# Queries as extra columns of the key products, absorbing products on column groups, and a new step order in a decoder-layer kernel

## The chip, the cores and the metric

The kernel runs on one core of a Trainium2 chip. The metric is device time in microseconds of one execution of the whole program; lower is better. The core has TensorE (PE in the profile, its weight loads PEld), VectorE (DVE), ScalarE (ACT), GpSimd (POOL) and a queue that issues DMAs (SP).

## What is computed

One layer of a decoder for 256 prompt tokens and 8 sequences with 4 new tokens each, in float32: an input projection, an mLSTM branch, a branch of latent attention (MLA), a merge, and a convolutional FFN. The change lies in the MLA branch. For the samples it computes, per sequence, over 1024 cached positions and the new ones:

```python
def mla_keys(c_kv, k_rope, w_uk, g_kn, g_kr):
    k_nope = jnp.einsum('...sc,chd->...shd', c_kv, w_uk)          # 512 latent -> 16 heads x 128
    k_r = jnp.broadcast_to(k_rope[..., None, :], k_nope.shape[:-1] + (B_ROPE,))
    return qk_norm(k_nope, k_r, g_kn, g_kr)                       # RMS norm of each head's 192 entries

def mla_attend(q, k, c_kv, mask, w_uv):
    s = jnp.einsum('bqhe,bkhe->bhqk', q, k).astype(jnp.float32) * ATTN_SCALE
    s = jnp.where(mask, s, -jnp.inf)
    p = jax.nn.softmax(s, axis=-1).astype(c_kv.dtype)
    o_lat = jnp.einsum('bhqk,bkc->bqhc', p, c_kv)
    return jnp.einsum('bqhc,chv->bqhv', o_lat, w_uv)
```

## The kernel before

**Precision.** A large product is made of three in the type fp32r: both operands are split into a high part (suffix H or hi) and a low part (L or lo), and hi·hi, hi·lo and lo·hi are added up in one PSUM bank. Small products are plain f32.

**Page loop (lines 1322 to 1880).** The cache of a sequence is 8 pages of 128 positions (`NPG`), and there are 8 sequences (`NB`): 64 pages. The keys' RMS norm needs the squares of all 16 heads' keys, so PE computes the keys of each page: `keys(b, j)` multiplies the page's turned latents (`latH`, `latL`, as weights) with `w_uk` (`ukH`, `ukL`, as moving columns) in 4 groups of 512 columns (4 heads), each group 4 chunks times 3 products in a PSUM bank of its own (0 to 3). ACT squares a group (`squares`, L1627), and DVE sums it per head (`sums`, L1701). The scores don't use these keys: the queries were multiplied with `w_uk` beforehand (`qlat`: 16 heads x 4 queries = 64 columns, high and low part), and `scores(b, j)` multiplies the same latents with 128 columns (L1480, high times both parts) and 64 columns (L1481, low times high), four of each, and adds the rotary part (L1482, f32, 64 rows of weights). Its bank 5 is folded by DVE (`fold`, L1709) into the buffer `sc`. For each page PE runs: `turn(b, j + 1)` (five f32 transposes of the next page, L1452 and L1453), `keys`, `scores`, and one small step for the sequence before (maxima, denominators, values L1555, turn_out L1560). After a sequence's 8 pages `scale` on DVE divides by the norms and takes maxima; for the last sequence this, the softmax and the value product come at the end with nothing beside them.

**Key loop of the prompt (L793 to 808 and the functions above it).** For `h` in 0 to 18, PE does: `keys(h)` (head h of the prompt's keys, L718, four f32 products of 288 columns), `flip(h - 2)` (transposes of one head of `w_uk`, L728), `absorb(h - 3)` (L736: 32 columns of sample queries as weights, 512 moving columns of the turned `w_uk`, f32, output on the 32 rows `(h % 4) * 32` of bank 6), every second head `key_sums` (L750), and every fourth `absorbed` (L743). DVE copies each turned head out of PSUM (`flipped`, L1232, two buffers), adds and inverts norms (`key_norm` L1236, `key_inverse` L1242) and copies four absorbed heads (`absorbed`, L1247). ACT copies and squares keys, and takes roots (`key_root`, L1014).

**Prompt attention.** Before it come two products with `w_uv`, new keys and the scores of four heads. Then for eight pairs of heads `step(p)`: `turn_p(2p)` (L859), `values(2p - 1)` (L869, L870), `turn_p(2p + 1)`, `values(2p)`, and after the step `scores(p + 2)` (L845, L849) and, in the first four, `values_of` (L829: 512 columns, f32). `turned_p`, `exps`, `scaled` and `out` are ACT's part, `soft` and `norm_` DVE's.

The order of work on an engine is the order of the code; engines meet at semaphores (`wait_ge`, `need`). The rest of the kernel (the projections, blocks of 288-column products at L298, L299, L303) is not touched.

## Time and profile before

| | |
|---|---|
| three runs | 2988.29, 2986.86, 2981.94 us; median 2986.86 us |
| the profiled execution | 2982.09 us, its span 2980.3 us |
| PE busy | 2918.2 us, 98% of the span |
| DVE, ACT busy | 1435.8 us (48%), 1121.8 us (38%) |
| granted TensorE clock, mean | 0.993 of 2.4 GHz |
| key loop and prompt attention | about 145 to 303 us |
| page loop | about 318 to 1184 us |

A PE row stands for a product with its drain; neighbours overlap, so the time that a product takes of PE is the distance between two starts, not its length. A plain f32 product appears as two rows. "PEld" rows are the loads of weights, which run beside products.

### The profile page before, as it was taken

How to read it: one execution, taken by the hardware profiler on the slowest of the kernel's cores; microseconds unless marked ns; L12 is line 12 of the kernel's file. 1: busy time of each engine (PE TensorE's matmuls, PEld its weight loads, DVE VectorE, ACT ScalarE, POOL GpSimd, SP SyncE). 2: the span in 40 equal slices, each digit the busy share in tenths (PEclk: the TensorE clock that was granted, in tenths of full speed). 3: DMA queues.
4: the chain of work that ended last, by engine and by line, in shares of the span. 5: the costliest groups of instructions: out<-in, count | busy, mean ns of one | idle time of the engine just before them, and what ended most of it. 6: DMA issues, size and time to landing. Idle time of an engine off the chain costs nothing. (4 is left out here: it accounts for less than half of the span.)

```text
span 2980.3 us, 49155 instructions
## 1 busy us (share of the span) xinstructions
PE 2918.2 (98%) x19158; PEld 2649.9 (89%) x19158; DVE 1435.8 (48%) x2153; ACT 1121.8 (38%) x1750; POOL 104.4 (4%) x346
## 2 busy tenths in 40 slices
PE   8998999999999999899999999999999999999999
PEld 7855788888888887899999999999999999999999
DVE  5464433333333333355545444445677654677644
ACT  5525322322322232354444333334444433444433
POOL 0000000000000000000000000002200000000100
PEclk9999899999999999999999999999999999999999
DMA  6512401011011001656565655556555555655564
GB/s 208 201 65 78 128 1 32 1 33 33 5 29 32 16 17 71 196 158 194 158 195 156 195 162 170 165 159 185 171 161 163 165 146 168 185 159 165 148 179 127
DMA packets 619380, 370.93 MB, mean 124 GB/s; under 512 B 23792, under 2 KB 600882, under 8 KB 618168
## 3 DMA queue, kind: packets, MB, share of 16 engines
q1 hardware_dynamic: 607032, 356.44, 40.4%
q10 hardware_dynamic: 11824, 11.50, 1.1%
q8 instruction: 109, 1.79, 0.2%
q0 software_dynamic: 368, 0.81, 0.1%
q14 instruction: 47, 0.39, 0.0%
HBM read 345.98 MB, written 22.75 MB: 124 GB/s over the span
## 5 line engine op out<-in xcount | busy, mean ns | idle before, releaser
L286 DVE TENSOR_TENSOR w_lo_b<-stage,w_hi_b 128x2048 fp32r<-128x2048 f32 (+1 forms) x289 | 619.1, 2142 | 429.1 <-ACT w_hi_b L279 429.0
L298 PE MATMUL bank<-xnH,w_hi_b 128*128 128x288 f32 x2784 | 755.9, 299 | 5.9 <-PEq L191 5.8
L299 PE MATMUL bank<-xnL,w_hi_b 128*128 128x288 f32 x2784 | 750.6, 296 | 0.0
L279 ACT ACTIVATE w_hi_b<-stage 128x2048 fp32r<-128x2048 f32 (+1 forms) x289 | 517.8, 1792 | 571.2 <-PE bank L303 536.7
L298 PEld LDWEIGHTS bank<-xnH,w_hi_b 128*128 128x128 f32 x2784 | 524.3, 188 | 18.3 <-issue 18.0
L299 PEld LDWEIGHTS bank<-xnL,w_hi_b 128*128 128x128 f32 x2784 | 523.9, 188 | 0.3
L1465 PE MATMUL bank<-ukH,latH 128*128 128x512 f32 x1024 | 405.2, 396 | 0.0
L1701 DVE TENSOR_REDUCE rk<-sq_n 128x4 f32<-128x512 f32 x256 | 175.5, 685 | 466.5 <-ACT sq_n L1627 466.5
L1467 PE MATMUL bank<-ukH,latL 128*128 128x512 f32 x1024 | 399.5, 390 | 0.0
L1466 PE MATMUL bank<-ukL,latH 128*128 128x512 f32 x1024 | 399.4, 390 | 0.0
L303 PE MATMUL bank<-xnH,w_lo_b 128*128 128x288 f32 x2784 | 396.5, 295 | 0.0
L303 PEld LDWEIGHTS bank<-xnH,w_lo_b 128*128 128x128 f32 x2784 | 378.1, 188 | 0.0
L1627 ACT ACTIVATE sq_n<-bank 128x512 f32<-128x512 f32 x256 | 153.2, 599 | 510.7 <-PE bank L1467 510.7
L298 PE MATMUL bank<-haH,w_hi_b 128*128 128x288 f32 x1024 | 278.1, 299 | 6.8 <-PEq L191 3.9
L299 PE MATMUL bank<-haL,w_hi_b 128*128 128x288 f32 x1024 | 276.6, 297 | 0.0
L1467 PEld LDWEIGHTS bank<-ukH,latL 128*128 128x128 f32 x1024 | 192.6, 188 | 40.7
L1466 PEld LDWEIGHTS bank<-ukL,latH 128*128 128x128 f32 x1024 | 193.0, 188 | 38.1
L1465 PEld LDWEIGHTS bank<-ukH,latH 128*128 128x128 f32 x1024 | 192.9, 188 | 38.1
L298 PEld LDWEIGHTS bank<-haH,w_hi_b 128*128 128x128 f32 x1024 | 194.3, 190 | 7.5 <-issue 7.3
L299 PEld LDWEIGHTS bank<-haL,w_hi_b 128*128 128x128 f32 x1024 | 195.1, 191 | 0.0
L303 PE MATMUL bank<-haH,w_lo_b 128*128 128x288 f32 x1024 | 151.9, 295 | 0.0
L303 PEld LDWEIGHTS bank<-haH,w_lo_b 128*128 128x128 f32 x1024 | 141.6, 188 | 0.0
(472 smaller groups left out, 3011.7 us busy)
## 6 DMA issues: line engine op xcount, KB each, us to landing
stage<-in_w_in_dram SPq DMA_DIRECT2D x88, 1024.0 KB, 5.2
stage<-in_w_up_dram SPq DMA_DIRECT2D x88, 1024.0 KB, 5.4
stage<-in_w_down_dram SPq DMA_DIRECT2D x64, 704.0 KB, 4.6
latf<-in_cache_kv_latent_dram SPq DMA_DIRECT2D x64, 256.0 KB, 2.5
stage<-in_w_branch_a_dram SPq DMA_DIRECT2D x16, 1024.0 KB, 5.5
stage<-in_w_branch_b_dram SPq DMA_DIRECT2D x16, 1024.0 KB, 5.5
stage<-in_w_out_dram SPq DMA_DIRECT2D x16, 1024.0 KB, 5.6
stage<-in_w_uk_dram SPq DMA_DIRECT2D x8, 1024.0 KB, 5.2
```

The source lines that it names most:

```text
L279: act.activation(h, a, ACT.Copy).then_inc(w_hi, 1)
L286: dve.tensor_tensor(lo, a, h.bitcast(F32), ALU.subtract).then_inc(w_lo, 1)
L298: pe.matmul(out, hi, xH(k), start=first and k == 0, stop=False)
L299: pe.matmul(out, hi, xL(k), start=False, stop=False)
L303: mm = pe.matmul(out, lo, xH(k), start=False, stop=last and k == kc - 1)
L1465: pe.matmul(bank[g][:], h, ukH[:, k, cols], start=k == 0, stop=False)
L1466: pe.matmul(bank[g][:], h, ukL[:, k, cols], start=False, stop=False)
L1467: mm = pe.matmul(bank[g][:], lo, ukH[:, k, cols], start=False, stop=k == LC - 1)
L1627: act.activation(sq[:, g % 2, :], bank[g][:], ACT.Square).then_inc(n_sq, 1)
L1701: dve.tensor_reduce(rk[:, b.mod(2), j, g * 4:g * 4 + 4], sq[:, g % 2, :].rearrange("p (h d) -> p h d", d=NOPE), AX.X, ALU.add).then_inc(n_ ...
```

## The change

1. **Queries as columns.** `ukH` and `ukL` get 128 columns more: two slots of 64, left and right of the first three heads. DVE copies the next sequence's `qlat` into a slot (`next_queries`, three copies, at the third page of a sequence). The page's key products now run in 5 groups: 3 heads and the queries (448 columns), three times 3 heads (384), and 4 heads (512), in banks 0, 1, 2, 3, 5. The scores fall out of group 0; `scores` and `fold` are gone, ACT copies the 64 score columns out of bank 0 before it squares the keys.
2. **Rope product first.** The rotary product (f32, 64 columns) stands at the head of group 0, right after the transposes.
3. **Absorbing products on column groups.** `absorb(j)` issues the products of four heads in a row, on the four groups of 32 output rows; the turned `w_uk` gets four buffers, two of them where `xnL` and `xnH` lie, so that `flipped(2)` and `flipped(3)` wait for the stores of those, and the store of `xnH` moves forward in SP's order. The copy of four absorbed heads moves from DVE to ACT, ahead of `key_root`.
4. **A new step order** in the prompt's attention, on PE and on ACT.
5. Some small buffers (`ol`, `hs`, `sq`) lie elsewhere.

```diff
@@ sync: the stores
-                    for i in range(6, VCH):
+                    chunk(6)
+                    sp.wait_ge(x_H, KC)
+                    sp.dma_start(xnH_dram, xnH[:].bitcast(F32)).then_inc(xH_out, 16)
+                    for i in range(7, VCH):
                         chunk(i)
-                    sp.dma_start(xnH_dram, xnH[:].bitcast(F32)).then_inc(xH_out, 16)
@@ tensor: key loop
-                    def absorb(h):
-                        g = h % 4
-                        pe.wait_ge(u_ev, h + 1)
-                        if g == 0:
-                            need(pe, u_ab, h // 4)
-                        mm = pe.matmul(bank[6][g * N_S:(g + 1) * N_S, :], smp[:, h, :], ukT[:, h % 2, :], start=True, stop=True)
+                    def absorb(j):
+                        pe.wait_ge(u_ev, 4 * j + 4)
+                        need(pe, u_ab, j)
...
+                        for g in range(4):
+                            mm = pe.matmul(bank[6][g * N_S:(g + 1) * N_S, :], smp[:, 4 * j + g, :], ukT[g], start=True, stop=True)
                         mm.then_inc(u_q, 1)
...
+                        if h >= 6 and h % 4 == 2:
+                            absorb(h // 4 - 1)
                         if 2 <= h < BH + 2:
                             flip(h - 2)
...
-                        if h >= 3:
-                            absorb(h - 3)
...
-                        if h >= 8 and h % 4 == 0:
-                            absorbed(h // 4 - 2)
+                        if h >= 7 and h % 4 == 3:
+                            absorbed(h // 4 - 1)
@@ tensor: step(p)
                         turn_p(2 * p + 1)
+                        if p < 4:
+                            values_of(2 + p // 2, p % 2)
+                        if p + 2 < PAIRS:
+                            scores(p + 2)
                         values(2 * p)
@@ scalar: end of the key loop
                     high_part(2)
+                    absorbed(3)
                     for i in range(PAIRS - 2, PAIRS):
                         key_root(i)
@@ scalar: step
                         turned_p(2 * p)
+                        if p:
+                            out(2 * p - 1)
+                        turned_p(2 * p + 1)
                         if p + 1 < PAIRS:
                             exps(2 * p + 2)
-                        if p:
-                            out(2 * p - 1)
-                        if p + 1 < PAIRS:
                             exps(2 * p + 3)
-                        turned_p(2 * p + 1)
-                        if p + 1 < PAIRS:
                             scaled(2 * p + 2)
-                        out(2 * p)
-                        if p + 1 < PAIRS:
                             scaled(2 * p + 3)
                         if p < 4:
                             values_of(2 + p // 2, p % 2)
+                        out(2 * p)
@@ vector: turned heads
-                        need(dve, u_q, h - 1)
-                        dve.tensor_copy(ukT[:, h % 2, :], bank[2 + h % 2][:]).then_inc(u_ev, 1)
+                        need(dve, u_q, h // 4)
+                        if h == 2:
+                            dve.wait_ge(xL_out, 16)
+                        if h == 3:
+                            dve.wait_ge(xH_out, 16)
+                        dve.tensor_copy(ukT[h % 4], bank[2 + h % 2][:]).then_inc(u_ev, 1)
@@ page loop
+            GROUPS = [(0, 3), (3, 6), (6, 9), (9, 12), (12, 16)]
+            KG = len(GROUPS)
...
                         pe.wait_ge(f_lo, b.of(NPG, j + 1))
-                        for g in range(4):
+                        pe.wait_ge(f_rt, b.of(NPG, j + 1))
+                        if j == 0:
+                            pe.wait_ge(q_slot, b.of(1, 1))
+                        for g in range(KG):
...
-                            need(pe, n_sq, b.of(4 * NPG, 4 * j + g - 3))
+                            need(pe, n_sq, b.of(KG * NPG, KG * j + g - KG + 1))
...
+                            if g == 0:
+                                pe.matmul(out[:, parts(s)[0]], rT[:, a, :], qrC[:, s, :], start=True, stop=False, skip_group_check=True)
                             for k in range(LC):
                                 h, lo = latH[:, a, k * P:(k + 1) * P], latL[:, a, k * P:(k + 1) * P]
-                                pe.matmul(bank[g][:], h, ukH[:, k, cols], start=k == 0, stop=False)
-                                pe.matmul(bank[g][:], h, ukL[:, k, cols], start=False, stop=False)
-                                mm = pe.matmul(bank[g][:], lo, ukH[:, k, cols], start=False, stop=k == LC - 1)
+                                pe.matmul(out, h, ukH[:, k, cols], start=g > 0 and k == 0, stop=False, skip_group_check=g == 0)
+                                pe.matmul(out, h, ukL[:, k, cols], start=False, stop=False, skip_group_check=g == 0)
+                                mm = pe.matmul(out, lo, ukH[:, k, cols], start=False, stop=k == LC - 1, skip_group_check=g == 0)
                             mm.then_inc(n_k, 1)
-                    def scores(b, j):
...
@@ scalar: squares
+                            if g == 0:
+                                q_, k_ = parts(b.mod(2))
+                                part = bank[0][:, k_]
...
+                                act.activation(sc[:, b.mod(2), j, :], bank[0][:, q_], ACT.Copy).then_inc(f_fold, 1)
@@ vector
-                    def fold(b, j):
...
+                    def next_queries(b):
+                        s = b.mod(2)
+                        dve.tensor_copy(qrC[:, s, :].rearrange("p (h q) -> p h q", q=S_S), qrS[:, :, bass.ds(b.of(S_S), S_S)])
+                        dve.tensor_copy(ukH[:, :, slot(s)], qlat[:, :, bass.ds(b.of(), 1), 0].rearrange("p k o h s -> p k (o h s)").bitcast(F32))
+                        dve.tensor_copy(ukL[:, :, slot(s)], qlat[:, :, bass.ds(b.of(), 1), 1].rearrange("p k o h s -> p k (o h s)").bitcast(F32)).then_inc(q_slot, 1)
```

**In the page loop, on PE,** the end of one page and the start of the next before (L1465 to L1467 are the key products, L1480 to L1482 the scores, L1452 and L1453 the transposes):

```order
1482 L1467 MATMUL bank<-ukH,latL 128x512
1483 L1480 MATMUL bank<-qlat,latH 128x128
1484 L1481 MATMUL bank<-qlat,latL 128x64
1485 L1480 MATMUL bank<-qlat,latH 128x128
1486 L1481 MATMUL bank<-qlat,latL 128x64
1487 L1480 MATMUL bank<-qlat,latH 128x128
1488 L1481 MATMUL bank<-qlat,latL 128x64
1489 L1480 MATMUL bank<-qlat,latH 128x128
1490 L1481 MATMUL bank<-qlat,latL 128x64
1491 L1482 MATMUL bank<-qrS,rT 128x64
1492 L1452 MATMUL bank<-cst,latf 128x128 x4
1493 L1453 MATMUL bank<-cst,latf 64x128
```

and the same place now (L1517 to L1519 the key products, L1514 the rotary one; `krr` is where `qrC` lies):

```order
1530 L1519 MATMUL bank<-ukH,latL 128x512
1531 L1495 MATMUL bank<-cst,latf 128x128 x4
1532 L1496 MATMUL bank<-cst,latf 64x128
1533 L1514 MATMUL bank<-krr,rT 128x64
1534 L1517 MATMUL bank<-ukH,latH 128x448
1535 L1518 MATMUL bank<-ukL,latH 128x448
1536 L1519 MATMUL bank<-ukH,latL 128x448
```

The eight short products are gone, the rotary one follows the transposes, and the key products are 12 of 448 columns, 36 of 384 and 12 of 512 where they were 48 of 512.

**In the key loop of the prompt, on PE,** before (heads 14 to 18):

```order
703 L718 MATMUL bank<-ckvT,stage 128x288 x4
704 L728 MATMUL bank<-cst,stage 128x128 x4
705 L736 MATMUL bank<-u_reg,xT_reg 32x512
706 L718 MATMUL bank<-ckvT,stage 128x288 x4
707 L728 MATMUL bank<-cst,stage 128x128 x4
708 L736 MATMUL bank<-u_reg,xT_reg 32x512
709 L750 MATMUL bank<-xT_reg,cst 128x512
710 L728 MATMUL bank<-cst,stage 128x128 x4
711 L736 MATMUL bank<-u_reg,xT_reg 32x512
```

and now, from the same head (L723 keys, L733 transposes, L744 absorbing products, L758 sums, L751 `absorbed`):

```order
698 L723 MATMUL bank<-ckvT,stage 128x288 x4
699 L744 MATMUL bank<-u_reg,xT_reg 32x512 x2
700 L744 MATMUL bank<-uk_58,xT_reg 32x512
701 L744 MATMUL bank<-uk_59,xT_reg 32x512
702 L733 MATMUL bank<-cst,stage 128x128 x4
703 L723 MATMUL bank<-ckvT,stage 128x288 x4
704 L733 MATMUL bank<-cst,stage 128x128 x4
705 L758 MATMUL bank<-xT_reg,cst 128x512
706 L751 MATMUL bank<-cst,u_reg 128x128 x4
707 L733 MATMUL bank<-cst,stage 128x128 x8
708 L758 MATMUL bank<-xT_reg,cst 128x512
709 L744 MATMUL bank<-u_reg,xT_reg 32x512 x2
```

One absorbing product a head became four in a row every four heads, and the last four stand behind everything else of the loop.

## Rows read from the trace of the kernel before

**Rows 1.** Busy time by stretch: length, each engine's busy us (count), granted clock, DMA share, GB/s.
```profile
186.00:218.00 32.00, 29.74 (x119) 16.44 (x118) 22.52 (x27) 8.57 (x29) 1.48 (x7) 1.00 0.20 66
218.00:230.00 12.00, 11.28 (x53) 4.82 (x52) 10.95 (x10) 1.53 (x4) 0.00 (x0) 1.00 0.30 90
282.00:304.00 22.00, 15.67 (x82) 11.39 (x80) 7.58 (x25) 13.99 (x45) 0.00 (x0) 0.92 0.30 96
800.00:900.00 100.00, 100.00 (x502) 81.83 (x501) 33.39 (x63) 28.79 (x66) 0.00 (x0) 1.00 0.09 24
```

**Rows 2.** Timeline of PE over one page: start us, length us, engine, line, operation.
```profile
898.72 0.27 PE L1453 MATMUL bank<-cst,latf 128*64 128x128 f32 x1
...
909.73 0.22 PE L1480 MATMUL bank<-qlat,latH 128*128 x1
...
910.46 0.24 PE L1481 MATMUL bank<-qlat,latL 128*128 x1
910.63 0.43 PE L1482 MATMUL bank<-qrS,rT 64*128 x2
911.00 0.22 PE L1505 MATMUL bank<-cst,psums 128*64 128x1 f32 x1
```

**Rows 3.** Timeline of PE, products of 288 columns (12 distances from the first to the last).
```profile
1293.37 0.29 PE L299 MATMUL bank<-xnL,w_hi_b 128*128 128x288 f32 x1
...
1294.97 0.30 PE L299 MATMUL bank<-xnL,w_hi_b 128*128 128x288 f32 x1
```

**Rows 4.** Timeline of PE two pages earlier: the rotary product and a like one behind it.
```profile
884.84 0.43 PE L1482 MATMUL bank<-qrS,rT 64*128 x2
885.11 0.38 PE L1501 MATMUL bank<-cst,mxw 64*128 64x64 f32 x2
```

**Rows 5.** Timeline of PE in the key loop; in brackets the wait before and its end.
```profile
178.35 1.02 PE L736 MATMUL bank<-u_reg,xT_reg 128*32 128x512 f32 x2 [1.13 <-DVE u_reg L1247]
179.30 1.12 PE L750 MATMUL bank<-xT_reg,cst 128*128 128x512 f32 x2
...
195.83 1.02 PE L736 MATMUL bank<-u_reg,xT_reg 128*32 128x512 f32 x2 [1.13 <-DVE u_reg L1247]
...
220.56 1.04 PE L736 MATMUL bank<-u_reg,xT_reg 128*32 128x512 f32 x2 [0.72 <-DVE u_reg L1232]
```

**Rows 6.** Timeline of PE, products with w_uv on four column groups.
```profile
1201.76 1.95 PE L1605 MATMUL bank<-stage,olat 128*32 128x128 f32 x64 [0.80 <-DVE olat L1764]
1203.50 1.96 PE L1605 MATMUL bank<-latf,olat 128*32 128x128 f32 x64
```

**Rows 7.** DVE's inversions and copies in the key loop: count, busy us, mean ns, idle before.
```profile
L1242 DVE RECIPROCAL rkb<-rkb 128x512 f32<-128x512 f32 x8 | 26.7, 3343 | 0.0
L1232 DVE COPY u_reg<-bank 128x512 f32<-128x512 f32 x16 | 10.9, 684 | 13.6 <-PE bank L728 13.6
```

**Rows 8.** Timeline of SP's queue: the last two loads of w_uq.
```profile
105.20 3.54 SPq L556 DMA_DIRECT2D stage<-in_w_uq_dram  x2
```

**Rows 9.** DMA issues: the store of xnH, KB and us to landing.
```profile
xnH_scratch<-xnH SPq DMA_DIRECT2D x1, 2304.0 KB, 12.7
```

**Rows 10.** Timeline of ACT: the split of the last w_uq chunk.
```profile
131.88 0.62 ACT L935 ACTIVATE w_hi_b<-stage 128x512 fp32r<-128x512 f32 x1
```

**Rows 11.** Timeline of the prompt's attention: a wait, the starts of steps 2 and 4, the end.
```profile
253.57 0.67 PE L869 MATMUL bank<-u_reg,vv 128*128 128x256 f32 x2 [0.62 <-ACT u_reg L1081]
...
260.49 0.49 PE L859 MATMUL bank<-cst,c_tok 128*128 128x128 f32 x3
...
279.26 0.49 PE L859 MATMUL bank<-cst,c_tok 128*128 128x128 f32 x3
...
303.16 0.38 ACT L1081 ACTIVATE u_reg<-bank 128x256 f32<-128x256 f32 x1 [1.07 <-PE bank L870]
```

**Rows 12.** Weight loads by line: count, busy us, mean ns, idle before.
```profile
L298 PEld LDWEIGHTS bank<-xnH,w_hi_b 128*128 128x128 f32 x2784 | 524.3, 188 | 18.3 <-issue 18.0
...
L1465 PEld LDWEIGHTS bank<-ukH,latH 128*128 128x128 f32 x1024 | 192.9, 188 | 38.1
```

More of the change, by code:

```diff
@@ L887, in _ @@
                         step(p)
-                        if p + 2 < PAIRS:
-                            scores(p + 2)
-                        if p < 4:
-                            values_of(2 + p // 2, p % 2)
                     values(BH - 1)
@@ L1020, in high_part, with absorbed @@
                             act.activation(qlat[:, k, :, 0, 4 * j:4 * j + 4, :], q_, ACT.Copy).then_inc(u_h, 1)
+                    def absorbed(j):
+                        act.wait_ge(u_q, j + 1)
+                        need(act, u_abt, j - 1)
+                        act.activation(ab[:, j % 2, :], bank[6][:], ACT.Copy).then_inc(u_ab, 1)
                     def latent_rows(t):
@@ L1674, in _ @@
                         act.wait_ge(uk_land[g], 16)
-                        act.activation(ukH[:, :, g * GC:(g + 1) * GC], uk_stage(g), ACT.Copy).then_inc(uk_hi, 1)
+                        for dst, src in uk_pieces(g):
+                            ins = act.activation(ukH[:, :, dst], uk_stage(g)[:, :, src], ACT.Copy)
+                        ins.then_inc(uk_hi, 1)
                     middle, end = batches(batch)
@@ L1773, in batch @@
                                 lo(b + 1, 0)
-                            if j >= 1:
-                                fold(b, j - 1)
                             sums(b, j)
+                            if j == 2 and not last:
+                                next_queries(b + 1)
                             if post and j == 0:
```

121 lines of the change are left out of this document (67 added, 54 removed).

## The prediction, written before the changed kernel was run

> **What bounds the kernel now.** The table comes first: PE is busy for 98% of the span, DVE and ACT for less than half. So the time is what PE is given to do, plus its waits. The table of stretches says where that holds. In the page loop PE is busy for all of 100 us, DVE for 33 and ACT for 29, at full clock [rows 1]: there PE alone counts, and every nanosecond taken off it 64 times over is time. At the end of the prompt's key loop PE is nearly full too, but DVE is busy for 22.5 of 32 us and then for 10.95 of 12: the second engine is close behind. At the end of the prompt's attention PE is busy for 15.7 of 22 us and ACT for 14.0, with the clock at 0.92: a chain over three engines. These are three different stages, and the change touches all three, so I cost them apart. The last views are PE's timelines in each, read by the distance between starts.
>
> **Page loop: what goes.** From the first score product to the end of the rotary one is 909.73 to 911.00, 1.27 us [rows 2]. The eight score products take 0.90 of it, 0.1125 each, though they have only 128 or 64 columns: 53 or 27 ns of columns at 2.4 GHz. They are paced by something a product pays anyway, which next to a wide product is hidden.
>
> **What comes.** Between 898.72 and 909.73 lie 48 products of 512 columns: 11.01 us, of which about 0.13 is the change from f32 to fp32r, so 0.2267 each [rows 2]. 512 columns at 2.4 GHz are 0.2133; the rest is 13.4 ns. Products of 288 columns are 0.1333 apart (twelve distances from 1293.37 to 1294.97): 0.120 plus 13.3 ns [rows 3]. So a product costs its columns plus 13.4 ns, between 288 and 512 columns at least. The new widths lie between: 448 columns 0.2001, 384 columns 0.1734. A page is 12 x 0.2001 + 36 x 0.1734 + 12 x 0.2267 = 11.36 us, against 48 x 0.2267 = 10.88: 0.48 more. The columns of a page are the same as before (25408); the gain is that no product is too short to hide its overhead.
>
> The rotary product stays, in a new place: 0.27 when an f32 product follows it [rows 4], 0.36 when the f32 run ends and other work comes [rows 2]. I take 0.25, since in the new order it stands within an f32 run already begun; the bounds are 0.20 and 0.36. The switch from fp32r to f32, which it paid before, now falls on the transposes: 0.08, by the gap of 0.17 before it against 0.11 between score products [rows 2]; bounds 0 and 0.1. Per page: -1.27 + 0.48 + 0.25 + 0.08 = -0.46. Times 64: **-29.5 us**. With the bounds, -0.59 to -0.33 a page, -38 to -21; I doubt the far ends, since they take all bounds at once, and use -34 to -24.
>
> **What hides the rest of it.** ACT gets a copy of 64 columns and a fifth square a page, DVE a fifth sum and, once a sequence, three copies, and loses the fold. Even 1.5 us a page more leaves both under half of a page of some 12 us [rows 1]. Five banks for five groups mean that a bank is written again a whole page after it was squared. The new waits of PE: for `f_rt` of a page turned one page ago, and for `q_slot`, filled five pages ahead; behind them all of PE is queued, but both have long been met. At the end of the last sequence the fold of DVE no longer stands before `scale`, but the last squares and sums now end as late as the fold did: nothing. I cost all these at nothing. At the loop's start DVE's three copies fill a wait for the first split of `w_uk`; if not, 1 us.
>
> **Key loop: PE's part.** An absorbing product costs 178.35 to 179.30, 0.95 us, and four heads 17.48 (178.35 to 195.83) with one wait of 1.13 for DVE's copy [rows 5]. Do four products on four groups of 32 output rows run at once? The products with `w_uv` do: 64 rows start within 1.74 us [rows 6], 32 products at two rows each, 54 ns for 128 columns of f32, and the plain price is four passes of 53 ns. So a group of four costs what one did, 0.93. PE saves 16 x 0.95 - 4 x 0.93 = 11.5, and the waits, three of 1.13 and one of 0.72 [rows 5], 4.1: **15.6 at most**. The Trainium skill is more careful ("TensorE: Matmul & The Clock Gate", Part 3): three column tiles gave it 2.38 times, not 3. At that efficiency a group would cost about 1.2 and the sum would be 1.1 smaller; the rows here show nearly four times.
>
> **Key loop: what is late next.** DVE. It has per two heads one inversion of 3.34 us, two copies of 0.68 and a sum of the same size, 5.4 with nothing in between [rows 7], and with PE at (17.48 - 1.13 - 3.80 + 0.93) / 2 = 6.7 per two heads it keeps up until the keys end. Then PE has only transposes left, and DVE still three inversions. The last four absorbing products now wait for the last turned head, whose copy stands behind an inversion on DVE. Laid out by hand from these durations, PE comes there at 205.0 and the copy is done at 208.5: a wait of 3.6. In ACT's order `key_root` of the last two pairs stands behind the copy of these products, which delays DVE's last inversions by 2 us but not PE, which has two `values_of` before. So **-12 us**; bounds -16 (no such wait) and -8 (the wait is doubled, or lets the clock fall, as it fell in the attention [rows 1]).
>
> The store of `xnH` is moved before the last chunk of `w_uq`. The two last chunks are issued from 105.2 to 108.7 now [rows 8]. A store issued at 105.7 that takes 12.7 us [rows 9] is done by 118.4; the chunk, a third of its bytes, would be there by 123 even if wholly behind it, and ACT wants it at 131.9 [rows 10]. The turned heads that wait for both stores come 25 us later still. Nothing.
>
> **Step order.** A step of the first kind takes 9.38 us (two from 260.49 to 279.26), with a wait of 0.62 for ACT and a smaller one [rows 11], and a slow start after each. In the new order `values_of` and `scores` stand where PE waited; the copy `out(2p)` now stands between `values(2p)` and `values(2p + 1)` with one set of transposes beside it, 0.3 left over. I take 0.8 for each of four steps. The last four take 279.26 to 303.54, 24.3 us, 6.1 a step [rows 11], of which ACT is busy for 14.0 / 22, 3.9 [rows 1]. The new order lets ACT do both heads' exponentials without waiting for PE between them; I take half of its 2.2 idle a step, near 1, as an estimate. Sum 3.2 + 3.8 = **-7 us**, bounds -9 and -3 (only the first four).
>
> **Sum.** -29.5 - 12 - 7 = -48.5. The profiled execution took 2982.1, so 2933.6; it is the fast end of the three runs (median 2986.9, mean with the profiled one 2984.8). From the middle of these, the change comes out at **2937**.
>
> **Rivals.**
>
> *The prompt stages give little.* DVE's chain and ACT's chain set the ends of the first two stages, and a faster PE only waits longer. For it: DVE at 10.95 of 12 us, ACT at 14.0 of 22 [rows 1]. Against: PE is nearly full before these ends. Key loop -6, steps -2, pages -29.5: 2948.
>
> *The prompt stages give all,* -16 and -9, and the pages -33: 2927.
>
> *The narrower products cost more than columns plus 13 ns.* A weight load lasts 0.188 us at 288 and at 512 columns alike [rows 12], longer than the 0.160 of 384 columns. If narrow products were paced by it, 36 x (0.188 + 0.013 - 0.173) = 1.0 more a page: -0.46 becomes +0.54, +35 in the loop, with the prompt's -19 then 3001, **slower**. It decides from 0.19 us a product of 384 columns on; at that the loop gains nothing and only the prompt's gain is left. Against it: the 288-column products, with the same load, are 0.133 apart [rows 3]. The Trainium skill speaks for a form of it (the same page, Part 3): loads overlap running products only if their row groups differ, and these do not. By that rule every product would pay its load, and a page with 61 products instead of 57 would be slower by four loads, 0.45 at the 0.1125 of the score products; the loop +29, and 2995. The spacing of the wide products, columns plus 13 ns, speaks against that too.
>
> *The turn costs more:* rotary product 0.36, switch 0.1, and 0.1 again when fp32r resumes: pages -19, and 2947.
>
> **How the numbers follow.** Forecast 2937 (own range 2928 to 2945) 0.55; prompt stages little 0.17; all gained 0.12; the turn costs more 0.08; slower 0.04; a wait that I overlooked eats most of it and leaves about 2975 to 2990, 0.04. The range reaches to both near rivals: 2923 to 2952. About 0.2%, 6 us, is what a measurement can tell from no change. Faster 0.94, same 0.02, slower 0.04.
>
> **What would show it.** In the profile after: the distance from a page's last transpose to the next page's down by 0.46; key products at 0.200, 0.173 and 0.227; the absorbing products' eight rows within about 0.9 us; a wait of 3 to 4 us before the last of them, ended by DVE's copy of a turned head; no wait for `values` in the first steps. The forecast is wrong if 384-column products stand 0.19 or more apart, if PE waits at a page's start, or if DVE's inversions in the key loop end as late as before (229 us).

## The result, and the profile after

The changed kernel takes 2963.77 us (median of three executions between 2961.59 and 2965.10; a fourth, at a granted clock of 0.65, took 4214.71 us and is left out), the kernel before 2986.09 in the same comparison. The ratio is 0.9926 (95% interval 0.9913 to 0.9940): 22 us faster, where 2937 was forecast, 49 us faster. The direction is right, the size is less than half, and the time lies above the range of 2923 to 2952.

The table splits the difference of the two profiled executions (spans 2980.3 and 2963.2) at places that both kernels have. "First key product" is the first wide product of page 0, "step 0" the first transpose of probabilities in the prompt's attention.

| stretch | before, us | after, us | difference | forecast |
|---|---|---|---|---|
| start to step 0 | 242.69 | 232.94 | -9.75 | -12 |
| the eight steps | 60.85 | 56.57 | -4.28 | -7 |
| end of the steps to the first key product | 14.47 | 15.26 | +0.8 | 0 |
| 63 distances from page to page | 853.91 | 845.02 | -8.9 | -29 |
| last page's keys | 10.78 | 11.38 | +0.6 | in the pages |
| last key product to the next stage's transposes | 22.69 | 26.05 | +3.4 | 0 |
| the rest | | | +1.1 | 0 |

The sum is -17.1 and not -22, since the profiled execution was the slowest of the three for the changed kernel and near the fastest for the kernel before. Two thirds of what is missing lie in the page loop: a page got 0.14 us shorter on the mean (853.91 / 63 = 13.554 against 13.413), and 0.12 to 0.13 once the first pages, which run at a lower clock, are left out, not 0.46. It is not the same for all pages: 0.20 to 0.25 where only products of 128 rows and columns lie between two pages' keys, 0.05 where `denominators` or `values` come in, and 0.08 longer where `spread` does.

One page of the changed kernel, in PE's timeline (start us, length us, engine, line, operation), to be read beside [rows 2]:

```profile
905.45 0.65 PE L1495 MATMUL bank<-cst,latf 128*128 128x128 f32 x4
905.95 0.27 PE L1496 MATMUL bank<-cst,latf 128*64 128x128 f32 x1
906.15 0.43 PE L1514 MATMUL bank<-krr,rT 64*128 64x64 f32 x2
906.51 0.47 PE L1517 MATMUL bank<-ukH,latH 128*128 128x448 f32 x1
906.82 0.36 PE L1518 MATMUL bank<-ukL,latH 128*128 128x448 f32 x1
...
909.05 0.33 PE L1517 MATMUL bank<-ukH,latH 128*128 128x384 f32 x1
...
915.31 0.39 PE L1517 MATMUL bank<-ukH,latH 128*128 128x512 f32 x1
...
918.16 0.65 PE L1594 MATMUL bank<-latf,sc_s 128*64 128x512 f32 x2
```

From the last transpose to the rotary product it is 0.20 us, from there to the first key product 0.36: 0.56, of which 0.03 would be there without it, so 0.53 where I had 0.25. The key products themselves are where they were expected: 36 of 384 columns in 6.26 us, 0.1739 each (forecast 0.1734); 12 of 448 columns in 2.54 with the change of type at the front; 12 of 512 columns in 2.85 with 0.09 behind them for the shape of `values` (64 output columns). Where the transposes come next there is nothing of the kind: the forecast's switch of 0.08 does not exist there.

PE in the key loop, to be read beside [rows 5]; in brackets the idle time before a row and what ended it:

```profile
169.51 0.62 PE L744 MATMUL bank<-u_reg,xT_reg 128*32 128x512 f32 x2
...
169.98 0.60 PE L744 MATMUL bank<-uk,xT_reg 128*32 128x512 f32 x2
170.51 0.66 PE L733 MATMUL bank<-cst,stage 128*128 128x128 f32 x4
...
188.86 0.63 PE L751 MATMUL bank<-cst,u_reg 128*128 128x128 f32 x4 [1.63 <-DVE qlat L1263]
...
203.50 0.63 PE L751 MATMUL bank<-cst,u_reg 128*128 128x128 f32 x4 [1.63 <-DVE qlat L1263]
...
209.15 0.65 PE L744 MATMUL bank<-u_reg,xT_reg 128*32 128x512 f32 x2 [3.29 <-DVE uk L1247]
```

Four absorbing products start within 0.5 us and the next work 1.00 behind them: four column groups do run at once, as [rows 6] let expect. The last row is the wait that was forecast, 3.29 against 3.6. The two rows with 1.63 are waits that I had not seen.

A lone absorbing product has a second price, which these groups show by its absence. First the kernel before, with one between transposes (L728) and keys (L718), then the changed kernel at a head without any:

```profile
173.07 0.60 PE L728 MATMUL bank<-cst,stage 128*128 128x128 f32 x4
173.60 1.05 PE L736 MATMUL bank<-u_reg,xT_reg 128*32 128x512 f32 x2
174.57 2.21 PE L718 MATMUL bank<-ckvT,stage 128*128 128x288 f32 x8
176.62 0.60 PE L728 MATMUL bank<-cst,stage 128*128 128x128 f32 x4
```

```profile
176.62 0.60 PE L733 MATMUL bank<-cst,stage 128*128 128x128 f32 x4
177.06 2.11 PE L723 MATMUL bank<-ckvT,stage 128*128 128x288 f32 x8
179.00 0.60 PE L733 MATMUL bank<-cst,stage 128*128 128x128 f32 x4
```

The transposes ahead of it take 0.53 instead of 0.44, and the keys behind it 2.05 instead of 1.94. So each change to products of 32 output columns and back costs up to 0.2 us beside the product (0.15 where transposes come behind it), and the kernel before makes it 16 times, the changed one four times.

What DVE does ahead of the second of these waits (its timeline):

```profile
199.27 3.34 DVE L1257 RECIPROCAL rkb<-rkb 128x512 f32<-128x512 f32 x1
202.53 0.82 DVE L1263 TENSOR_TENSOR qlat<-bank,qlat 128x128 fp32r<-128x128 f32 x4
```

`low_part` (L1263) frees the bank that PE's next transposes write, and it stands behind an inversion of 3.34 us.

### The profile page after: what moved, and what is told of

Its sections match the earlier page's. It is cut to its first block and busy times, and to the rows that moved or that the text cites. A ratio compares the mean times of both kernels' runs of the same rounds, so it can differ in the third digit from the quotient of the medians.

```text
span 2963.2 us, 49885 instructions
## 1 busy us (share of the span) xinstructions
PE 2902.8 (98%) x19414; PEld 2701.2 (91%) x19414; DVE 1430.0 (48%) x2174; ACT 1142.6 (39%) x1883; POOL 105.3 (4%) x346
## 5 line engine op out<-in xcount | busy, mean ns | idle before, releaser
L1517 PE MATMUL bank<-ukH,latH 128*128 128x384 f32 (+2 forms) x1280 | 457.9, 358 | 0.0
L1519 PE MATMUL bank<-ukH,latL 128*128 128x384 f32 (+2 forms) x1280 | 452.3, 353 | 0.0
L1518 PE MATMUL bank<-ukL,latH 128*128 128x384 f32 (+2 forms) x1280 | 451.8, 353 | 0.0
L1748 DVE TENSOR_REDUCE rk<-sq_n 128x3 f32<-128x384 f32 (+1 forms) x320 | 184.8, 579 | 508.0 <-ACT sq_n L1672 508.0
L1672 ACT ACTIVATE sq_n<-bank 128x384 f32<-128x384 f32 (+1 forms) x320 | 163.9, 512 | 443.0 <-PE bank L1519 443.0
L1517 PEld LDWEIGHTS bank<-ukH,latH 128*128 128x128 f32 x1280 | 240.8, 188 | 16.9
L1519 PEld LDWEIGHTS bank<-ukH,latL 128*128 128x128 f32 x1280 | 240.6, 188 | 14.4
L1518 PEld LDWEIGHTS bank<-ukL,latH 128*128 128x128 f32 x1280 | 240.9, 188 | 13.0
```

The lines of the kernel that those rows point to most:

```text
L1517: pe.matmul(out, h, ukH[:, k, cols], start=g > 0 and k == 0, stop=False, skip_group_check=g == 0)
L1518: pe.matmul(out, h, ukL[:, k, cols], start=False, stop=False, skip_group_check=g == 0)
L1519: mm = pe.matmul(out, lo, ukH[:, k, cols], start=False, stop=k == LC - 1, skip_group_check=g == 0)
L1672: act.activation(sq[:, (j + g) % 2, 0:(h1 - h0) * NOPE], part, ACT.Square).then_inc(n_sq, 1)
L1748: dve.tensor_reduce(rk[:, b.mod(2), j, h0:h1], sq[:, (j + g) % 2, 0:(h1 - h0) * NOPE].rearrange("p (h d) -> p h d", d=NOPE), AX.X, ALU.add ...
```

## The experiments

Two theories stood at the start for the page loop. **Theory A**: a product that uses 64 of the array's 128 rows, among products that use all, costs a change going in and another coming out, wherever it stands. **Rival B**: the price is that of an f32 product, or of its new place. Times are medians, with the ratio to the kernel before and its 95% interval; where there is one execution there is no interval.

### The rotary product with 128 rows

```diff
-            qrC = krr2[0:ROPE, 0:2, 1, :]
-            rT = sb(ph, "rT", [ROPE, 2, P])
+            qrC = krr2[:, 0:2, 1, :]
+            rT = sb(ph, "rT", [P, 2, P])
...
+                    dve.memset(rT[ROPE:, :, :], 0.0).then_inc(rt_zero, 1)
```

> The changed kernel with its rotary product as a product of 128 rows: the weights rT have 64 more rows of zeros, so the sum is the same. In the changed kernel the stretch from the first transpose of a page to its first key product is 0.56 us, where I had 0.28. Theory A (the cost is a change of the array's row height before and after a 64-row product): the distance from the rotary product to the first key product falls from 0.36 to about 0.15 (four passes of 64 columns, 0.107, plus a change of type), a page gets 0.2 to 0.3 shorter, the kernel 13 to 19 us shorter than the changed one, near 2948. Rival B (the cost is that of an f32 product of any height among others, or of its place): 0.36 stays, 2964. Rival C (the wider load costs more): longer.

Measured: 2942.18 us, ratio 0.9857 (0.9841 to 0.9874), 21.6 us less than the changed kernel; 13.080 us a page against 13.413. The same place in its timeline:

```profile
906.24 0.27 PE L1497 MATMUL bank<-cst,latf 128*64 128x128 f32 x1
906.35 0.33 PE L1515 MATMUL bank<-krr,rT 128*128 128x64 f32 x2
906.50 0.45 PE L1518 MATMUL bank<-ukH,latH 128*128 128x448 f32 x1
```

0.20 has become 0.11 and 0.36 has become 0.15, with twice the rows and the same sum. That is 0.09 for going into the 64 rows and 0.21 for coming out; the first key product is 0.02 quicker as well. Theory A holds, and slightly more was gained than it had said.

### No rotary product

```diff
-                            if g == 0:
-                                pe.matmul(out[:, parts(s)[0]], rT[:, a, :], qrC[:, s, :], start=True, stop=False, skip_group_check=True)
```

> The changed kernel without the rotary product, so the scores lack their rotary part; all else stays. It gives the whole price of that product. Theory A: its price in the page is about 0.5, so a page is 0.5 shorter and the kernel some 32 us shorter than the changed one, 2932. The forecast's term (0.25, and the switch of 0.08 remains with the transposes): 16 us, 2948.

Measured: 2928.29 us, ratio 0.9816 (0.9799 to 0.9832); 12.861 us a page. Its scores lack the rotary part. So the product costs 13.413 - 12.861 = 0.55 us a page, 35 us in all, where the forecast had 0.25 and 16. The first key product now starts 0.03 behind the last transpose:

```profile
909.00 0.27 PE L1496 MATMUL bank<-cst,latf 128*64 128x128 f32 x1
909.03 0.45 PE L1515 MATMUL bank<-ukH,latH 128*128 128x448 f32 x1
909.32 0.36 PE L1516 MATMUL bank<-ukL,latH 128*128 128x448 f32 x1
```

### The rotary product in fp32r, with 64 rows

```diff
+        krr2_at = nc.sbuf_base - 4 * 6 * ROPE
...
-            qrC = krr2[0:ROPE, 0:2, 1, :]
-            rT = sb(ph, "rT", [ROPE, 2, P])
+            qrC = nc.alloc_sbuf_tensor_at("qrR", [P, 3, 2, ROPE], F32R, offset=krr2_at)[0:ROPE, 0:2, 1, :]
+            rT = sb(ph, "rT", [ROPE, 2, P], F32R)
```

> The changed kernel with the rotary product in fp32r instead of f32, still of 64 rows (so it computes with rounded operands). Theory A: the passes shrink from 0.107 to 0.027 us, the changes of row height stay: a page is about 0.08 shorter, 5 us in all. Rival B (the f32 form is what costs): a page is 0.25 or more shorter, 16 us.

Measured: 2953.49 us in one run; 13.274 us a page, 0.139 less than 13.413.

```profile
914.57 0.27 PE L1497 MATMUL bank<-cst,latf 128*64 128x128 f32 x1
914.77 0.29 PE L1515 MATMUL bank<-qrR,rT 64*128 64x64 f32 x1
915.00 0.47 PE L1518 MATMUL bank<-ukH,latH 128*128 128x448 f32 x1
```

The way in stays at 0.20, the same as with f32, and the way out falls from 0.36 to 0.23. The value lies between the two expectations, 0.08 and 0.25: the f32 form costs 0.14, more than its passes, but the larger part, 0.33 with 128 rows, is the row height. The Trainium skill has the rule ("TensorEngine Tiling (Array Packing)", Key Properties): a change of the tiling mode drains the engine. It gives no price, and it does not say that a plain product of 64 rows is such a change; the runs here fit that reading, and going in and coming out cost 0.3 us together. I had not weighed it.

### The kernel before with this one edit

```diff
-        qrS = sb(kept, "qrS", [ROPE, BH, N_S])
+        qrS = sb(kept, "qrS", [P, BH, N_S])
...
-            rT = sb(ph, "rT", [ROPE, 2, P])
+            rT = sb(ph, "rT", [P, 2, P])
...
+                    dve.memset(qrS[ROPE:], 0.0).then_inc(rt_zero, 1)
+                    dve.memset(rT[ROPE:], 0.0).then_inc(rt_zero, 1)
```

> The kernel before with one edit: its rotary product has 128 rows, with zeros in the 64 new rows of both operands. Nothing of the change is in it. Theory A (a 64-row product among products of 128 rows costs 0.31 us, wherever it stands): a page is about 0.3 us shorter, 0.27 to 0.33, the kernel 18 to 21 us shorter than before, 2964: this one edit gives about as much as the whole change. Rival (the price belongs to the new place, between transposes and key products; in the old place the 0.27 that I read from the rows holds): under 0.1 a page, 2978 or more.

Measured: 2975.72 us, ratio 0.9977 (0.9966 to 0.9989): 7 us, not 18 to 21. A page is 0.170 shorter on the mean, 13.385 against 13.554; that makes 10.7 us in the profiled execution, the fastest of seven that lie between 2971.82 and 2980.98, so this total is known less well than the others. The eight pages of a sequence differ. First a page whose neighbours use the whole array, then one with `spread` behind the rotary product:

```profile
890.75 0.24 PE L1482 MATMUL bank<-qlat,latL 128*128 x1
890.83 0.41 PE L1483 MATMUL bank<-qrS,rT 128*128 x2
891.08 0.61 PE L1453 MATMUL bank<-cst,latf 128*128 128x128 f32 x4
```

```profile
448.57 0.41 PE L1483 MATMUL bank<-qrS,rT 128*128 128x64 f32 x2
448.92 0.43 PE L1502 MATMUL bank<-cst,mxw 64*128 64x64 f32 x2
449.28 0.65 PE L1453 MATMUL bank<-cst,latf 128*128 128x128 f32 x4
```

On the four pages of the first kind (a transpose of 128 rows, `turn_out` or the next turn behind it) the way in falls from 0.17 to 0.08, the way out from 0.36 to 0.25, the transposes behind it from 0.49 to 0.44, and the page by 0.22 to 0.29. Where `spread` (64 rows), `denominators` or `values` (64 output columns) come next, the change of shape only moves behind the rotary product: 0.35 from 448.57 to 448.92, where it was 0.27 before [rows 4]. Those pages gain 0.1 or nothing. So A is right about the mechanism, but my expectation counted it on eight pages where it works in full on four. The new place is thus worth something after all: there the neighbours are always products of 128 rows, and 128 rows gain 0.33 on each page.

### The parts apart

`prompt_only` is the kernel before with the prompt's part, `loop_only` with the page loop's part; the edits are those of the diff above. `steps_only` has from it only the order of `step` and of ACT's loop.

> The kernel before with the prompt's part of the change alone: the absorbing products in fours, ACT's copy of them, the earlier store of xnH, the new step order. The page loop is as before. Theory (the trace of the changed kernel: the page loop begins 14.1 us earlier): 13 to 15 us shorter than the kernel before, near 2970. Rival (the two parts help or hurt each other, for instance the page loads of the loop come too late for an earlier start): under 11 us.

> The kernel before with the page loop's part of the change alone. Theory: 0.12 to 0.13 us a page, 8 us, less the 3.3 us that the stretch behind the last key product is longer in the changed kernel: 4 to 6 us shorter than the kernel before, near 2979. The forecast had 29.5 us. If the longer stretch behind the last keys is chance and not the change's, 8 us.

> The kernel before with the new order of the steps alone, in PE's and ACT's programs. Theory (the trace of the changed kernel): from the start of step 0 to that of step 4 34.3 us instead of 36.6, and the last four steps 22.3 instead of 24.3, so 4.3 less. The forecast had 3.2 and 3.8. Rival (a part of the gain came with the other start of this stage): under 3 in all.

Measured: `prompt_only` 2969.76 us, ratio 0.9948 (0.9932 to 0.9965), 14.5 us; `loop_only` 2979.22, ratio 0.9978 (0.9967 to 0.9989), 5.0 us by the medians and 6.6 by the ratio. The product of the two ratios is 0.9926, that of the whole change: the parts neither help nor hurt each other. The page loop's part, which carried 29.5 of 48.5 in the forecast, brings a quarter to a third of the two gains. `steps_only` took 2980.07 in its one run; its trace has 34.31 us from step 0 to step 4 (before 36.57) and 21.58 for the last four (before 24.28), 5.0 in all. The rival, under 3 and dependent on the other part, falls by the trace; the total in one run is too coarse to say more.

### DVE's order in the key loop

```diff
-                        if h >= 6 and h % 2 == 0:
-                            key_inverse(h // 2 - 3)
                         if h >= 10 and (h - 10) % 4 == 0:
                             low_part((h - 10) // 4)
+                        if h >= 6 and h % 2 == 0 and h < 16:
+                            key_inverse(h // 2 - 3)
+                        if h == 17:
+                            key_inverse(5)
+                    key_inverse(6)
```

ACT's last two `key_root` move ahead of `absorbed(3)` as well.

> The changed kernel with another order on DVE and ACT in the prompt's key loop: low_part stands ahead of key_inverse, the sixth key_inverse behind the copy of the last turned head, and ACT's last two key_root ahead of its copy of the last absorbing products. Theory: the waits of PE of 1.63, 1.63 (at the transposes of absorbed heads) and 3.29 us (at the last absorbing products) are DVE's order, so they go and step 0 of the attention starts about 5 us earlier than in the changed kernel (227 to 229 instead of 232.9). Rival: DVE's whole work is the bound, the waits only move to the attention's first softmax or to key_norm, and step 0 starts within 1.5 us of where it did.

Measured: 2956.95 us, ratio 0.9905 (0.9888 to 0.9921), 6.8 less than the changed kernel. Step 0 starts at 226.77, 6.2 earlier than 232.94. The sum of the three waits was 6.55, and 1.5 of waiting is left; the clock, which fell in the changed kernel behind the 3.29 (0.62 from 210 to 214 us), stays at 1.00 here, and the work that ran at the lower clock there was 1.6 us longer for it. The waits of PE that are left between 160 and 310 us (line and releaser, us in total, times, longest):

```profile
PE bank L875 <- ACT u_reg L1095: 3.1, 10, 0.6
PE bank L1498 <- DMA latf<-in_cache_k_rope_dram: 2.8, 1, 2.8
...
PE bank L733 <- DVE u_reg L1247: 1.3, 1, 1.3
...
PE bank L744 <- DVE uk L1247: 0.3, 1, 0.3
```

DVE's whole work is not the bound: the same instructions in another order make five of the 6.55 us go. A part comes back at the door of the page loop, where the first page's data now land 2.8 us after PE wants them (1.3 in the changed kernel).

### The stretch behind the last keys

This stretch is 3.4 us longer in the profile after, and the forecast had nothing for it. The granted clock is its difference. First before, then after (stretch, length, busy us of PE, weight loads, DVE, ACT, POOL with counts, granted clock, DMA share, GB/s):

```profile
1190.00:1194.00 4.00, 2.30 (x7) 0.77 (x8) 2.06 (x4) 0.77 (x2) 0.00 (x0) 0.50 1.02 438
...
1198.00:1202.00 4.00, 2.08 (x23) 1.44 (x25) 1.54 (x6) 0.00 (x0) 0.00 (x0) 1.00 0.00 0
1202.00:1206.00 4.00, 3.87 (x131) 3.44 (x122) 0.42 (x1) 0.48 (x2) 0.00 (x0) 1.00 0.01 4
```

```profile
1168.00:1172.00 4.00, 2.30 (x8) 0.87 (x10) 2.07 (x4) 0.77 (x2) 0.00 (x0) 0.50 1.02 435
...
1176.00:1180.00 4.00, 2.88 (x16) 1.54 (x13) 0.92 (x2) 0.00 (x0) 0.00 (x0) 0.87 0.00 0
1180.00:1184.00 4.00, 3.20 (x52) 3.04 (x55) 0.62 (x4) 0.00 (x0) 0.00 (x0) 0.50 0.00 0
```

Both kernels fall to the lower level (1.2 GHz) within PE's long wait for the maxima, 4.07 us before and 5.17 after; the changed one falls a second time, and the products with `w_uv` run in it. Four kernels put products that nobody reads into PE's waits there:

```diff
+                    def warm(n):
+                        for x in range(n):
+                            pe.matmul(bank[7][:, 0:GC], latH[:, 1, 0:P], latL[:, 1, :], start=True, stop=True)
+                    warm(22)
                     maxima(At(NB - 1))
+                    warm(2)
                     spread(At(NB - 1))
+                    warm(7)
                     values(At(NB - 1), 0, NJ, last=True)
                     last_denominators(At(NB - 1))
+                    warm(4)
```

`warm_short` has five such products ahead of `maxima`, `warm_first` the 22 alone, `warm_late` the last four alone.

> The changed kernel with products that nobody reads in PE's waits behind the last key product: 22 of 512 columns ahead of the transpose of the maxima, then 2, 7 and 4. In the changed kernel this stretch runs at a granted clock of 0.67, 0.50, 0.55, 0.87, 0.50 and 0.77 and takes 26.05 us to the last transposes, before 22.5. Theory (PE's waits let the clock fall, and the fall costs what the work behind it runs slower): with the waits filled the clock stays at 1.0 and the stretch takes 19 to 21 us, so 5 to 7 us less in all. Rival (the clock falls for another reason, or DVE and ACT set this stretch): 25 us or more.

> The changed kernel with five products of 512 columns, 1.13 us, behind the last key product, which nobody reads: as long as the score block that stood there before. Theory (the longer stretch behind the last keys, 26.05 against 22.5, comes from PE being idle 5.17 us there instead of 4.07, so the clock falls earlier and once more): 22 to 23.7. Rival (the score block has nothing to do with it, the second fall comes from when the clock happens to be looked at): 26, or a value between 22 and 26 that does not follow the idle time.

> The changed kernel with only the last four of the products that filled PE's waits behind the last keys: 0.9 us at full clock, between the last denominators and the products with the pair matrix, where PE waits 1.12 us. Theory (the second fall of the clock, 1180 to 1187 in the changed kernel, comes from the row of small waits there, 1.12 and 0.80 us): no second fall, the stretch takes 22.5 to 23.5 us instead of 26.05. Rival (the second fall does not come from this wait, it follows the first fall after a time): the fall stays and the stretch takes 25.5 or more.

> The changed kernel with only the first 22 of these products, in PE's wait of 5.17 us behind the last key product. Theory (the long wait makes the first fall, the later waits make the second): no first fall, so the products of values run at full clock, 3.6 us instead of 6.3; a second fall may come. 22.5 to 24 us for the stretch. Rival (the clock falls only after long idle time in sum, so filling the long wait alone keeps it up to the end): 20.5 to 21.5.

Measured, from the start of the last key product to the first of the next stage's transposes, in one trace of each kernel. "Clock back" is when the first fall ended, counted from that last key product:

| kernel | stretch, us | clock back, us | second fall |
|---|---|---|---|
| before / with the wide rotary product | 22.7 / 22.6 | 13.3 / 13.1 | no |
| warm_late | 22.7 | 13.4 | no |
| group_at / no_rope / steps_only | 23.4 / 23.7 / 23.9 | 11.7 / 12.0 / 12.4 | short |
| prompt_only / rope_r | 24.0 / 24.1 | 12.7 / 12.8 | short |
| loop_only / after | 26.0 / 26.05 | 14.1 / 14.4 | yes |
| wide_rope / warm_short / dve_order | 26.2 / 26.2 / 26.3 | 14.7 / 14.7 / 14.8 | yes |
| warm_first | 24.8 | 13.2, low from 9.8 only | yes |
| warm_tail / best | 20.3 / 20.3 | no fall | no |

`warm_tail` takes 2958.19 us, ratio 0.9908 (0.9891 to 0.9924), 5.6 less than the changed kernel. Its clock is 1.00 in all of the stretch, for instance in

```profile
1168.00:1172.00 4.00, 3.97 (x19) 2.18 (x21) 2.07 (x4) 0.78 (x2) 0.00 (x0) 1.00 1.02 435
1172.00:1176.00 4.00, 4.00 (x20) 1.46 (x16) 0.79 (x2) 0.00 (x0) 0.00 (x0) 1.00 0.60 258
```

and `warm_late`, with 0.9 us of filling in one place, has the first fall but not the second:

```profile
1172.00:1176.00 4.00, 4.00 (x14) 0.95 (x10) 0.00 (x0) 0.00 (x0) 0.00 (x0) 0.76 0.39 166
1176.00:1180.00 4.00, 3.20 (x33) 2.29 (x36) 1.54 (x6) 0.00 (x0) 0.00 (x0) 1.00 0.00 0
1180.00:1184.00 4.00, 3.88 (x125) 3.41 (x116) 0.42 (x1) 0.67 (x2) 0.00 (x0) 1.00 0.01 4
```

What is shown is that with PE's waits filled the clock stays up and the stretch takes 20.3 us, in two kernels, and that the total follows. Filling the long wait alone was not enough: `warm_first` fell all the same, later and shorter, and then a second time, so neither of its two expectations holds. `warm_short` put as much work in front of the long wait as the score block used to, and changed nothing.

What makes the second fall is not settled. In the changed kernel it comes with the small waits around `turn_out`, 1.12 and 0.80 us; the same two waits are in the kernel before ([rows 6] shows the 0.80), and there the clock stays. `warm_late` filled the first of them and has no second fall, but its clock was back 1.0 us earlier than in the changed kernel (13.4 against 14.4), ahead of the four products, and just where it was in the kernel before. So its expectation came true and still proves little. The table as a whole goes by that moment: back by 11.7 to 12.8 us, a short second fall; 13.1 to 13.4, none; 14.1 to 14.8, a full one. `group_at` differs from the changed kernel only in the order of the page's groups and lost 0.7 us against the kernel before, not 3.4; `prompt_only` and `steps_only` have the old loop and lost 1.3 and 1.2. So the 3.4 us are no fixed price of the change; they go with the moment at which the clock came back, as far as one trace of each kernel tells.

### The order of the groups

```diff
-            GROUPS = [(0, 3), (3, 6), (6, 9), (9, 12), (12, 16)]
+            GROUPS = [(0, 3), (3, 7), (7, 10), (10, 13), (13, 16)]
```

> The changed kernel with the group of four heads second instead of last: groups of 3, 4, 3, 3 and 3 heads. The 512-column products are now 0.2304 apart on the mean, but 0.227 where the moving columns start at a multiple of 2048 bytes (k = 3) and 0.230 to 0.235 elsewhere (k = 0, 1, 2); before all start at such a multiple, and all are 0.227 apart. With the new order this is so for k = 0 alone. Theory (the place of the moving columns sets the spacing): now the products of k = 0 are the fast ones. Rival (something beside the place, such as the engines that are busy at the page's end): the last products stay the odd ones, or all are 0.227.

Measured: the 512-column products of k = 1 and 2 are 0.228 and 0.227 apart, in the changed kernel 0.230 both (means over 62 pages); those of k = 0 are as fast, once the 0.002 that the first products of a group carry in both kernels is taken off. So the columns' place by k does not set it, and the theory falls. The group's place in the page and its place in memory both moved here, so which of them counts is not shown. The page is no shorter for it, 13.41 us, and the one run gave 2964.51. What makes the last group's products 3 ns longer stays open; it is 0.04 us a page.

### The best version

`wide_rope`, `dve_order` and `warm_tail` in one kernel.

> The changed kernel with three of the edits tried here at once: the rotary product of 128 rows, the order of DVE and ACT in the key loop, the products that fill PE's waits behind the last keys. Apart they gave about 21, 7 and 6 us. Theory (three places that don't touch): 2929 to 2933, 51 to 55 us shorter than the kernel before. Rival (the key loop's gain is lost where the first pages land later than PE comes to them, 2.8 us of waiting there already): 2933 to 2937.

Measured: 2929.83 us, ratio 0.9821 (0.9805 to 0.9837): 53 us faster than the kernel before, where the change alone brings 22. The three gains add up (21.6, 6.8 and 5.6 off 2963.8 would be 2929.8). PE still waits 2.4 us for the first page's data, so the door of the page loop is what is late next in the prompt.

## Why the prediction was wrong, point by point

**The rotary product: the step that failed.** "I take 0.25, since in the new order it stands within an f32 run already begun." I had two prices in the rows, 0.27 and 0.36, and explained their difference by the type of what follows. The rows say something else: in [rows 4] the next product, L1501, reads "64*128", it uses 64 rows as well; in [rows 2] the next one uses 128 rows, and there the way out of the 64 rows is paid. The 0.17 ahead of it in [rows 2] I booked as a switch of type; 0.09 of it is the way into 64 rows. In the page the product cost 0.50 before (0.09 on the way in, 0.36, and 0.05 at the transposes behind it), and it costs 0.53 now. Moving it gained nothing, while my sum took off all of its old price and gave back 0.25: 0.28 a page, 18 us. What the runs show in its place is a change of the array's shape on either side of the product: 0.33 us a page go when it gets 128 rows (`wide_rope`), and 0.22 to 0.29 in the kernel before where the neighbours use the whole array (`before_wide`).

**The gain of the wide products** was right in kind: eight score products went, 1.27 - 0.45 = 0.82. The key products with the query columns cost 0.58 more instead of 0.48 (11.65 - 0.09 against 11.01 - 0.03, both with the change to fp32r): 512 columns stand 0.2304 apart instead of 0.2267, 448 at about 0.204 instead of 0.200. Where only the turn comes next, the account is -0.82 - 0.50 + 0.58 + 0.53 = -0.21, and the trace has -0.20 to -0.22. On the other pages the rotary product used to share its change of shape with `spread`, `denominators` or `values`, which stood next to it. Now each pays alone, the last key product stands 0.32 instead of 0.23 ahead of them, and that takes another 0.15 to 0.3 off the gain, 0.09 on the mean of a sequence's eight pages. No term of the forecast had this. Together: -0.46 forecast, +0.28 for the rotary product, +0.10 for the key products, -0.08 for the switch that is not there, -0.05 for the transposes, which no longer stand behind 64 rows, +0.09 for what was shared, -0.12 measured.

**The slow rival** (products paced by their weight load, from 0.19 us for 384 columns on) is wrong: they stand 0.1739 apart with loads of 188 ns. The form of it that rests on the Trainium skill ("TensorE: Matmul & The Clock Gate", Part 3, loads overlap only where row groups differ) is wrong here too; the rule that mattered was the other one, on changes of mode.

**The rival "the turn costs more"** had the right place and nearly the right size: 0.36 for the rotary product and two switches of 0.1 make 0.56, where 0.53 was measured. Its sum is added up wrongly, though: with these terms a page is -1.27 + 0.48 + 0.56 = -0.23, which is -15 in the loop and 2951, not -19 and 2947. That is close to the pages where only the turn comes next (-0.20 to -0.22). It got there by the wrong terms: there is no switch at the transposes and none of 0.1 more when fp32r resumes, and the way into 64 rows is not in it. It had a chance of 0.08.

**The key loop**, -12 forecast, -9.75 measured. The products in fours cost 1.00 a group (0.93), the wait at the end 3.29 (3.6). Overlooked were the two waits of 1.63 for `low_part`. The new place of `absorbed`, one head later and four at once, puts PE's transposes just behind the inversion; I had laid DVE's order out by hand only for the last group. Filled in, the sum would be -12 + 3.3, about -9, but two more terms were missing and nearly cancel. The clock fell behind the wait of 3.29, and the work up to 219 us took 1.6 longer (1.46 instead of 1.00 for the last group, 8.16 instead of 6.97 for `values_of`). And twelve changes of shape fewer, at 0.15 to 0.2 each, gave about 2 back: the same mechanism as in the page loop, on the winning side here. That the stage came out near its forecast is in part luck.

**The steps**, -7 forecast, -4.3 measured, and -5.0 alone. 3.2 for the first four rested on a step of 9.38, but step 0 took 8.42 before (242.69 to 251.11), since it has no `values` of a head before it, and it gained nothing; the other three gained 0.75 each. In the new order `values` still waits 0.24 for ACT in each. 3.8 for the last four was half right (2.0): ACT stands idle there still, and PE waits 1.89 for it once.

**Hidden work** was hidden: the store of `xnH`, ACT's and DVE's added copies, `f_rt`, `q_slot`, the bank of the fifth group. PE is busy for all 100 us from 800 to 900, with ACT at 30.77 and DVE at 34.17.

**The clock** was left out. I named it as a risk of the forecast wait, and there it fell indeed: 0.62 of full speed from 210 to 214 us. The larger effect in the profiled execution came where nothing was changed, 3.4 us behind the last keys.

## What to carry to other kernels

Price a product by its neighbours' shape as well as by its own: a 64-row product among products of 128 rows cost 0.3 us more here than the same product filled up with 64 rows of zeros, and the added rows of zeros cost no time that shows. When a row of the profile is used as a price, read the rows on both sides of it, since the way in stands in the gap before and the way out in the gap behind. And where work is moved on one engine, lay out the other engine's queue for every place at which a bank is handed over, not only for the last.

## What was unexpected of the hardware

- The way into 64 rows took 0.09 us and the way out 0.11 (to f32 transposes) or 0.21 (to wide fp32r products). A change to products of 64 output columns costs the same on the way in: the last key product stands 0.32 ahead of `denominators` and `values`, 0.23 ahead of transposes. With 32 output columns it was 0.09 on the way in and 0.10 on the way out.
- An f32 product of 64 columns cost 0.14 us more than an fp32r one between the same neighbours.
- The clock fell to 1.2 GHz again (granted 1.00 from 1177 to 1179 us, 0.50 from 1179 to 1185) where PE's longest wait since it had come back was 1.12 us. The same waits left it alone in the kernel before, and the same tail took 22.6 to 26.3 us in kernels that differ only elsewhere.
- Products of 512 columns stood 0.230 apart as the last group of a page and about 0.228 as the second, for k = 1 and 2; why is open.
